# Last stage of a diffusion-step kernel: row moments on ScalarE, scale and finish on VectorE, inverse root on GpSimd

## The chip, the cores and the metric

The kernel runs on one core of one Trainium2 chip. A time is the device time of one execution in microseconds (us); the number to be forecast is the median over several executions. The core has TensorE (PE, matrix products, results in PSUM), VectorE (DVE), ScalarE (ACT), GpSimd (POOL), SyncE (SP, whose queue issues most of the DMAs) and 16 DMA engines. The engines run side by side, each works through its own instructions in order, and they wait for one another on semaphores.

## What is computed

One layer of a diffusion trunk on 1152 tokens (1024 latent, 128 context), width 1024, in float32. Cut to the parts that the change touches:

```python
def rms_norm(x, gain):
    y = xf * lax.rsqrt(jnp.mean(xf * xf, axis=-1, keepdims=True) + EPS)
    return (y * gain).astype(x.dtype)

def layer_norm(x, gain, bias):
    xc = xf - jnp.mean(xf, axis=-1, keepdims=True)
    var = jnp.mean(xc * xc, axis=-1, keepdims=True)
    return xc * lax.rsqrt(var + EPS) * gain + bias

hyo = rms_norm(hyo.reshape(B, L, HY_GROUPS, HY_GROUP_DIM), hy_out_gain)     # 8 groups of 64
x = layer_norm(DEEPNORM_ALPHA * x + g1 * mix, ln1_g, ln1_b)
moe = hier_moe(x * (1 + sc2) + sh2, ...)        # 2 of 32 experts for each token
x = layer_norm(DEEPNORM_ALPHA * x + g2 * moe, ln2_g, ln2_b)
```

## The kernel before

The tokens are nine tiles of 128 rows, eight latent (NLAT) and one context tile (NTILE = 9). The program runs through stages: modulation and projections, the Hyena convolution by Fourier matrices, the attention, the output projection with the first layer norm and the routing, a loop over blocks of 128 token rows through one expert each (33 blocks here), and the last stage, which adds each token's two expert rows to its residual and takes the second layer norm. Each engine's program is written out by hand in one function; nothing reorders it. `own` on VectorE, and `link` and `step` on GpSimd, issue one instruction and wait for its end before the next; `give` does the same on a named semaphore.

**Attention.** There are 72 rounds, eight heads for each of nine query tiles. In round i VectorE takes the maximum of the scores of round i + 1 (`maximum`, L1856), copies transposed probabilities out of PSUM (L1880) and, in round 8t + 7, takes the mean squares of the Hyena output of tile t: `mean_hyena`, one reduction of 512 columns to 8 sums (L1864) and one small operation (L1865). Its input, the squares, comes from ScalarE in round 8t + 4. In round 8t + 15 it also scales the attention output of tile t (`scale_attention`, L1527). GpSimd waits for the mean squares and for eight exponents (L636), then for ScalarE's copy of the attention's square sums (L639, round 8t + 11), takes the inverse roots in a chain of small steps (L642 to L648) and scales the Hyena rows (L651). TensorE turns the probabilities, multiplies with the values, and computes the scores of the next rounds, which wait until VectorE's maximum has freed their place in PSUM.

**Last stage.** SP waits until all expert rows are in HBM, then issues eight loads in four parts: tile 0, tiles 1 and 2, tiles 3 to 5, tiles 6 to 8. TensorE adds the two rows of a token by products with the identity, four for each tile of 128 x 1024, into one of four places `mixed(t)` in PSUM (AN = 4 places of two banks). VectorE adds ALPHA times x1 in place (`axpy`, L1540), takes the moments by two BatchNorm operations and an aggregation (L2081, L2082), and after every second tile takes the inverse roots of both in twelve small steps and one more for the bias (L2084, L1545, L1527, L1552, L1553, L2086). ScalarE then normalises from PSUM into one of three buffers `ynorm` (L1037) and thereby frees the place in PSUM. GpSimd multiplies with the gain and adds the bias (L751, L754) for the eight latent tiles; VectorE does so for the last. SP stores each tile to the output, and each buffer waits for its store before it is used again.

The last pair of expert products ends ahead of this stage, and between them and the first loaded tile TensorE has nothing to do.

## Time and profile before

| | us |
|---|---|
| median of 3 runs (1804.16 to 1805.94) | 1805.81 |
| the profiled execution | 1808.29 |
| its span on the page | 1806.1 |
| PE busy in the span | 1480.4 |
| DVE busy | 1015.0 |
| ACT busy | 358.9 |
| POOL busy | 365.7 |

The span runs from the first to the last instruction that the profile shows; the profiled execution took 2.2 us more than its span and 2.5 us more than the median. Changes are worked out as differences within the span and then taken off the median. A row of a timeline has its start, its duration, the engine and line, the operation with its output and input, how many instructions it merges, and in brackets the engine's idle time before it with what ended it. PSUM operands read PS, SBUF operands buffer.

### The profile page before, as it was taken

Reading aid. Unit: us, or ns where it says so; the run is one execution under the profiler, and the core shown is the slowest. Engines: PE = TensorE matmul, PEld = TensorE weight load, DVE = VectorE, ACT = ScalarE, POOL = GpSimd, SP = SyncE. Lnnn points to the kernel's source line nnn. Section 1 sums busy time; section 2 is a strip of 40 time slices with the busy share of each in tenths; the row PEclk is TensorE's granted clock in tenths of the full one; section 3 lists DMA queues with packets and bytes.
Section 4 is the critical chain, followed back from the end, with each engine's and each line's share of the span. In section 5 each row is a group of like instructions: output and inputs, shape, how many; then the busy total and the mean of one; then the engine's idle time right before and its main releaser. Section 6 shows DMA issues by size and latency. Waiting matters only on the chain.

```text
span 1806.1 us, 21613 instructions
## 1 busy us (share of the span) xinstructions
PE 1480.4 (82%) x8098; PEld 1008.3 (56%) x8098; DVE 1015.0 (56%) x1590; ACT 358.9 (20%) x665; POOL 365.7 (20%) x509
## 2 busy tenths in 40 slices
PE   7699998999974902924999997999469999999963
PEld 3466765444431401403888885455368888888821
DVE  3867882665538689587666662434533333333348
ACT  2544231111110100103565453000000000000001
POOL 0332030111100000000011114765212222222126
PEclk9799999999996955967999997999669999999986
DMA  9312203322311200202000003111248999998752
GB/s 302 135 58 80 85 30 134 117 94 94 117 64 37 83 13 19 75 12 103 1 2 2 1 2 140 58 59 47 93 167 318 325 334 329 333 339 315 248 232 88
DMA packets 96833, 229.50 MB, mean 127 GB/s; under 512 B 12439, under 2 KB 59095, under 8 KB 87992
## 3 DMA queue, kind: packets, MB, share of 16 engines
q1 hardware_dynamic: 72840, 195.14, 30.5%
q0 software_dynamic: 10960, 20.80, 3.3%
q10 hardware_dynamic: 12960, 12.59, 2.1%
q8 instruction: 46, 0.75, 0.2%
q14 instruction: 27, 0.22, 0.0%
HBM read 203.94 MB, written 40.01 MB: 135 GB/s over the span
## 4 chain that ended last, share of the span: by engine, by line
PE 68%; DVE 17%; DMA 4%; issue 4%; POOL 3%; ACT 3%; SPq 0%; ACTq 0%; DVEq 0%; POOLq 0%
PE PS L1047 57%; DVE buffer L1527 10%; PE PS L1050 6%; PE PS L1344 4%; DVE buffer L1540 2%; DMA buffer<-in_w_mod 2%; PE PS L1076 2%; POOL buffer L613 1%; POOL buffer L609 1%; DMA buffer<-expert_outputs 1%; DVE buffer L1856 1%; ACT buffer L977 1%; PE PS L1361 1%; ACT buffer L809 1%; DMA filter_spectra<-buffer 0%
## 5 line engine op out<-in xcount | busy, mean ns | idle before, releaser
L1047 PE MATMUL PS<-buffer 128*128 128x128 f32 (+5 forms) x5226 | 1235.4, 394 | 215.6 <-DVE buffer L1527 149.3
L1047 PEld LDWEIGHTS PS<-buffer 128*128 128x128 f32 (+1 forms) x5226 | 795.8, 197 | 627.4 <-issue 399.8
L1527 DVE TENSOR_TENSOR buffer<-buffer 128x512 f32<-128x512 f32 (+16 forms) x489 | 311.3, 637 | 28.2 <-ACT buffer L801 5.6
L1050 PE MATMUL PS<-buffer 128*128 128x128 f32 x1176 | 166.3, 284 | 63.7 <-DVE buffer L1527 53.5
L1527 DVE TENSOR_TENSOR buffer<-PS,buffer 128x1024 f32<-128x1024 f32 (+2 forms) x99 | 91.7, 927 | 188.8 <-PE PS L1047 168.2
L1050 PEld LDWEIGHTS PS<-buffer 128*128 128x128 f32 x1176 | 137.6, 155 | 93.8 <-issue 79.1
L1527 DVE TENSOR_TENSOR buffer<-buffer,PS 128x256 f32<-128x256 f32 (+3 forms) x53 | 27.4, 516 | 210.9 <-PE PS L1047 201.0
L1856 DVE TENSOR_SCALAR_CACHE_REDUCE buffer<-PS 128x1152 f32<-128x1152 f32 (+1 forms) x72 | 89.2, 1239 | 43.8 <-PE PS L1047 43.5
L944 ACT ACTIVATE buffer<-buffer 128x1152 f32<-128x1152 f32 (+1 forms) x72 | 83.7, 1163 | 109.8 <-DVE buffer L1856 109.8
L636 POOL TENSOR_TENSOR buffer<-buffer 128x8 f32<-128x8 f32 x9 | 1.8, 203 | 443.6 <-DVE buffer L1865 443.6
L1540 DVE SCALAR_TENSOR_TENSOR buffer<-buffer 128x512 f32<-128x512 f32 (+5 forms) x114 | 88.3, 774 | 3.9
L1025 ACT ACTIVATE buffer<-PS 128x256 f32<-128x256 f32 x33 | 12.7, 384 | 370.2 <-PE PS L1047 259.2
L1344 PE MATMUL PS<-buffer 128*64 128x128 f32 x1168 | 79.3, 279 | 6.4 <-ACT buffer L977 1.5
L1880 DVE COPY buffer<-PS 128x640 f32<-128x640 f32 x64 | 52.8, 825 | 55.0 <-issue 28.5
L1804 DVE TENSOR_SCALAR buffer<-PS,buffer 128x1024 f32<-128x1024 f32 (+1 forms) x24 | 21.0, 877 | 105.6 <-PE PS L1047 105.1
L1344 PEld LDWEIGHTS PS<-buffer 128*64 128x64 f32 x1168 | 62.6, 137 | 21.1 <-ACT buffer L977 15.2
L2061 DVE SCALAR_TENSOR_TENSOR buffer<-PS,buffer 128x1024 f32<-128x1024 f32 x33 | 42.4, 1284 | 40.5 <-PE PS L1047 40.5
L621 POOL TENSOR_TENSOR buffer<-buffer 2x256 f32<-2x256 f32 x16 | 12.0, 748 | 234.3 <-ACT buffer L779 234.3
L720 POOL COPY buffer<-buffer 128x1 int32 x32 | 5.9, 186 | 232.0 <-DVE buffer L2061 232.0
L2045 DVE COPY buffer<-PS 128x1024 f32<-128x1024 f32 x33 | 40.4, 1225 | 16.1 <-PE PS L1050 16.1
L711 POOL DMA_INDIRECT expert_outputs<-buffer x36 | 36.5, 1013 | 47.7 <-POOL buffer L720 25.5
L607 POOL TENSOR_TENSOR buffer<-buffer 128x256 f32<-128x256 f32 x8 | 8.7, 1088 | 174.3 <-ACT buffer L801 174.3
(150 smaller groups left out, 916.4 us busy)
## 6 DMA issues: line engine op xcount, KB each, us to landing
buffer<-in_exp_w_gate SPq DMA_DIRECT2D x33, 1024.0 KB
buffer<-in_exp_w_up SPq DMA_DIRECT2D x33, 1024.0 KB
buffer<-in_exp_w_down SPq DMA_DIRECT2D x33, 1024.0 KB
buffer<-in_w_mod SPq DMA_DIRECT2D x24, 1024.0 KB, 6.3
filter_spectra<-buffer ACTq DMA_DIRECT2D x88, 128.0 KB, 1.7
buffer<-filter_spectra SPq DMA_DIRECT2D x22, 512.0 KB, 3.6
buffer<-in_w_in SPq DMA_DIRECT2D x9, 1024.0 KB, 5.3
buffer<-expert_outputs SPq DMA_DIRECT2D x4, 1536.0 KB, 18.2
```

Source lines behind the costliest of these rows:

```text
L711: pool.indirect_dma_start(out=y_d[:, :], out_offset=bass.IndirectOffsetOnAxis(ap=rows, axis=0), in_=ybuf[:, s, :], in_offset=None, bounds_ ...
L944: act.activation(probs[:, i % 2, 0:n], probs[:, i % 2, 0:n], ACT.Exp, bias=nmax[:, i:i + 1], scale=-1.0, accum_out=psums[:, i:i + 1]).then ...
L1047: return nc.tensor.matmul(out, lhsT, rhs, start=start, stop=stop)
L1050: return nc.tensor.transpose(out, in_, ident)
L1076: last = nc.tensor.matmul(PS[32 * j:32 * j + 32, at:at + CHUNK], cond_wide[:, k, :], mod_weights(c)[:, k, :], start=half == 0, stop=half = ...
L1344: last = nc.tensor.matmul(PS[HD * u:HD * (u + 1), at:at + P], vals, probsT[:, (first + u) % 4, a, :], start=a == 0, stop=a == len(tiles) - ...
L1527: return dve.tensor_tensor(out, a, b, op)
L1540: own(dve.scalar_tensor_tensor(out, a, s, b, ALU.mult, op))
L1856: give(dve.tensor_scalar(probs[:, i % 2, 0:n], PS[:, 0:n], -1.0, None, ALU.mult, ALU.min, accum_out=nmax[:, i:i + 1]), "max_ready")
L1880: give(dve.tensor_copy(probsT[:, i % 4, 4:9, :], PS[:, 2048:2688].rearrange("p (t n) -> p t n", t=5)), "probsT_d")
L2045: dve.tensor_copy(xgT[:, s, :, :], PS[:, 0:1024].rearrange("p (k n) -> p k n", k=KT)).then_inc(sem("xT_ready"), 1)
L2061: dve.scalar_tensor_tensor(ybuf[:, s, :], PS[:, 2048:3072], row_scale[:, s, 0:1], row_gain, ALU.mult, ALU.mult).then_inc(sem("y_ready_to_s ...
```

## The change

In the attention, `mean_hyena` leaves VectorE. GpSimd waits for the squares and adds them up by halves, in six additions of 8 x 32, 8 x 16, 8 x 8, 8 x 4, 8 x 2 and 8 x 1 elements, followed by the small operation with 1/64 and EPS, all ahead of its wait for the exponents.

In the last stage:

- TensorE adds the residual of tiles 0 to 3, by two products each of a matrix ALPHA x identity with x1. These stand ahead of the waits for the loads. VectorE makes that matrix in the routing, in `upper`, by one operation on 128 x 128.
- VectorE adds the residual of tiles 4 to 8 as before (`add_residual`).
- ScalarE takes the moments: for each tile one Copy and one Square of 128 x 1024 from PSUM with an accumulated sum (`take_moments`). What they write is not read.
- VectorE computes (x - mean) x gain out of PSUM into the place of the loaded rows (`gain_rows`), which frees the place in PSUM for TensorE, and later multiplies with the inverse root and adds the bias, in SBUF (`finish_rows`).
- GpSimd takes the inverse roots in 17 small steps for each of the groups of tiles (0), (1, 2), (3, 4), (5, 6); VectorE those of tiles 7 and 8.
- The outputs are stored from the place of the loaded rows, so no buffer waits for a store.

```diff
             for t in range(NTILE):
                 v, r, tmp = (stat[:, i, 0:16] for i in range(3))
+                pool.wait_ge(sem("mix_squared"), t + 1)
+                y = mix_sq[:, 1, :].rearrange("p (g d) -> p g d", g=8)
+                n = HD // 2
+                while n > 1:
+                    link(pool.tensor_tensor(y[:, :, 0:n], y[:, :, 0:n], y[:, :, n:2 * n], ALU.add))
+                    n //= 2
+                link(pool.tensor_tensor(v[:, 8:16], y[:, :, 0], y[:, :, 1], ALU.add))
+                pool.sem_inc(sem("mix_meant"), 1)
+                link(pool.tensor_scalar(v[:, 8:16], v[:, 8:16], 1.0 / HD, EPS, ALU.mult, ALU.add))
                 pool.wait_ge(sem("exp_ready"), 8 * t + 8)
-                pool.wait_ge(sem("mix_meant"), t + 1)
...
+            for t0, t1 in GROUPS:
+                mean, square, v, r, tmp = (x[:, t0:t1] for x in (row_mean, row_square, row_var, row_scaling, row_tmp))
+                pool.wait_ge(sem("moments_taken"), 2 * t1)
+                step(pool.tensor_tensor(tmp, mean, mean, ALU.mult))
+                step(pool.tensor_tensor(v, square, tmp, ALU.subtract))
...
+                for scale in (1.0, 2.0, 16.0):
+                    step(pool.tensor_tensor(tmp, r, r, ALU.mult))
...
+            def take_moments(t):
+                if t < AN:
+                    act.wait_ge(sem("outputs_mixed"), t + 1)
+                else:
+                    act.wait_ge(sem("residual_added"), t - AN + 1)
+                if t:
+                    act.wait_ge(sem("moments_taken"), 2 * t)
+                act.activation(unread[:, 0, :], mixed(t), ACT.Copy, scale=1.0 / D, accum_out=row_mean[:, t:t + 1]).then_inc(
+                    sem("moments_taken"), 1)
+                act.activation(unread[:, 1, :], mixed(t), ACT.Square, scale=D ** -0.5, accum_out=row_square[:, t:t + 1]).then_inc(
+                    sem("moments_taken"), 1)
...
+            for t in (0, 1, 3, 2):
+                if t == 2:
+                    pe.wait_ge(sem("y_ready_to_send"), 2 * pairs + 2)
+                for h in range(2):
+                    mm(mixed(t)[:, 512 * h:512 * (h + 1)], upper, x1[:, t, 512 * h:512 * (h + 1)], True, False)
...
-                    pe.wait_ge(sem("ynorm_ready"), t - AN + 1)
+                    pe.wait_ge(sem("y_gained"), t - AN + 1)
...
+            def add_residual(t):
+                dve.wait_ge(sem("outputs_mixed"), t + 1)
+                dve.scalar_tensor_tensor(mixed(t), x1[:, t, :], ALPHA, mixed(t), ALU.mult, ALU.add).then_inc(sem("residual_added"), 1)
+
+            def gain_rows(t):
+                dve.wait_ge(sem("moments_taken"), 2 * t + 2)
+                dve.scalar_tensor_tensor(y_of(t), mixed(t), row_mean[:, t:t + 1], ln2_g, ALU.subtract, ALU.mult).then_inc(
+                    sem("y_gained"), 1)
+
+            def finish_rows(t):
+                dve.wait_ge(sem("y_gained"), t + 1)
+                dve.scalar_tensor_tensor(y_of(t), y_of(t), row_scaling[:, t:t + 1], ln2_b, ALU.mult, ALU.add).then_inc(
+                    sem("y_ready"), 1)
+
             dve.wait_ge(sem("ln2_loaded"), 32)
-            dve.wait_ge(sem("ynorm_ready"), NTILE)
-            own(tt(y, y, ln2_g, ALU.mult))
-            give(tt(y, y, ln2_b, ALU.add), "last_y_ready")
+            for t in range(NTILE):
+                if AN <= t:
+                    add_residual(t)
+                if t:
+                    gain_rows(t - 1)
+                if t in (3, 5, 7, 8):
+                    g = (3, 5, 7, 8).index(t)
+                    dve.wait_ge(sem("rows_scaling_ready"), g + 1)
+                    for done in range(*GROUPS[g]):
+                        finish_rows(done)
+            gain_rows(NLAT)
...
+            rsqrt(r, v, tmp)
+            for t in (NLAT - 1, NLAT):
+                finish_rows(t)
```

The order of VectorE's instructions in round 15 of the attention (tile 1) before the change. Rows give line, operation, output and input, and the semaphores waited for.

```order
L1880 COPY buffer<-PS 128x640 [waits attn_product,probs_transposed,max_ready]
L1864 TENSOR_REDUCE buffer<-buffer 128x8 [waits scales_ready,mix_squared,probsT_d]
L1865 TENSOR_SCALAR buffer<-buffer 128x8 [waits dve_step]
L1527 TENSOR_TENSOR buffer<-buffer,PS 128x512 [waits scales_spread,mix_meant]
L1856 TENSOR_SCALAR buffer<-PS 128x1152 [waits probs_transposed,scores_ready,attn_scaled]
```

And the same place after it (the helper line L1527 is now L1550, L1880 is L1894, L1856 is L1879):

```order
L1894 COPY buffer<-PS 128x640 [waits attn_product,probs_transposed,max_ready]
L1879 TENSOR_SCALAR buffer<-PS 128x1152 [waits probs_transposed,scores_ready,probsT_d]
L1894 COPY buffer<-PS 128x640 [waits attn_product,probs_transposed,max_ready]
L1550 TENSOR_TENSOR buffer<-buffer,PS 128x512 [waits scales_spread,probsT_d]
L1879 TENSOR_SCALAR buffer<-PS 128x1152 [waits probs_transposed,scores_ready,attn_scaled]
```

The reduction and the small operation are gone from between the copy and the next maximum.

VectorE in the last stage before the change, one tile and the inverse roots of a pair:

```order
L1540 SCALAR_TENSOR_TENSOR PS<-buffer,PS 128x1024 [waits outputs_mixed,dve_step]
L2081 BN_STATS buffer<-PS 128x6 [waits dve_step] x2
L2082 BN_AGGR buffer<-buffer 128x2 [waits dve_step]
L2084 TENSOR_SCALAR buffer<-buffer 128x2 [waits dve_step]
L1545 TENSOR_SCALAR buffer<-buffer 128x2 [waits dve_step]
L1527 TENSOR_TENSOR buffer<-buffer 128x2 [waits dve_step] x2
L1552 SCALAR_TENSOR_TENSOR buffer<-buffer 128x2 [waits dve_step]
```

And after it, from the residual of tile 5 to the residual of tile 7 (L2088 is `add_residual`, L2092 `gain_rows`, L2097 `finish_rows`):

```order
L2088 SCALAR_TENSOR_TENSOR PS<-buffer,PS 128x1024 [waits outputs_mixed]
L2092 SCALAR_TENSOR_TENSOR buffer<-PS,buffer 128x1024 [waits moments_taken]
L2097 SCALAR_TENSOR_TENSOR buffer<-buffer 128x1024 [waits y_gained,rows_scaling_ready]
L2097 SCALAR_TENSOR_TENSOR buffer<-buffer 128x1024 [waits y_gained]
L2088 SCALAR_TENSOR_TENSOR PS<-buffer,PS 128x1024 [waits outputs_mixed]
L2092 SCALAR_TENSOR_TENSOR buffer<-PS,buffer 128x1024 [waits moments_taken]
L2088 SCALAR_TENSOR_TENSOR PS<-buffer,PS 128x1024 [waits outputs_mixed]
```

The chain of small steps is gone from VectorE, and wide operations with waits for three other engines stand in its place.

TensorE at the end of the expert products, after the change; the wait for `yg_loaded0` is that for the first loaded tile:

```order
L1065 MATMUL PS<-buffer 128x512 [waits hidden_ready,y_ready_to_send]
L1065 MATMUL PS<-buffer 128x512 x9
L1516 REGISTER_ALU
L1065 MATMUL PS<-buffer 128x512 [waits y_ready_to_send]
L1065 MATMUL PS<-buffer 128x512
L1065 MATMUL PS<-buffer 128x512 [waits yg_loaded0]
L1065 MATMUL PS<-buffer 128x512 x3
```

Before the change the first row and three more products were followed at once by the wait for `yg_loaded0`; eight products now stand between.

## Rows read from the trace of the kernel before

**Rows 1.** The page: shares of the span in the chain that ended last.
```profile
PE 68%; DVE 17%; DMA 4%; issue 4%; POOL 3%; ACT 3%; SPq 0%; ACTq 0%; DVEq 0%; POOLq 0%
```

**Rows 2.** Timeline of DVE in the last stage, one pair of tiles.
```profile
1761.57 1.23 DVE L1540 SCALAR_TENSOR_TENSOR PS<-buffer,PS 128x1024 f32<-128x1024 f32 x1
...
1767.71 2.23 DVE L1545 TENSOR_SCALAR buffer<-buffer 128x2 int32<-128x2 int32 x1
1769.98 2.39 DVE L1527 TENSOR_TENSOR buffer<-buffer 128x2 f32<-128x2 f32 x2
...
1774.17 1.23 DVE L1540 SCALAR_TENSOR_TENSOR PS<-buffer,PS 128x1024 f32<-128x1024 f32 x1
```

**Rows 3.** Timeline of all engines in the last stage, POOL's row at that pair.
```profile
1767.57 2.35 POOL L751 TENSOR_TENSOR buffer<-buffer 128x1024 f32<-128x1024 f32 x1
```

**Rows 4.** The same timeline, the end of the program.
```profile
1798.15 1.20 ACT L1037 ACTIVATE buffer<-PS,buffer 128x1024 f32<-128x1024 f32 x1 [9.08 <-DVE buffer L2086]
1799.48 2.48 DVE L1527 TENSOR_TENSOR buffer<-buffer 128x1024 f32<-128x1024 f32 x2 [1.37 <-ACT buffer L1037]
1801.99 0.33 SPq L441 DMA_DIRECT2D out_ctx<-buffer  x1
```

**Rows 5.** The same timeline, PE: tiles 0 to 2, 3 to 4, one weight load.
```profile
1733.97 12.49 PE L1047 MATMUL PS<-buffer 128*128 128x512 f32 x24 [11.38 <-DMA buffer<-expert_outputs]
...
1748.19 7.13 PE L1047 MATMUL PS<-buffer 128*128 128x512 f32 x16 [1.73 <-DMA buffer<-expert_outputs]
...
1763.90 0.34 PEld L1047 LDWEIGHTS PS<-buffer 128*128 128x128 f32 x1 [0.52 <-issue]
```

**Rows 6.** Stretches of PE's work: busy us (count) by engine, granted clock, DMA share, GB/s.
```profile
1748.20:1758.80 10.60, 10.56 (x24) 4.47 (x24) 9.80 (x14) 2.30 (x2) 8.61 (x4) 1.00 0.64 258
1762.90:1768.80 5.90, 5.88 (x7) 2.51 (x8) 5.62 (x9) 0.97 (x1) 5.82 (x3) 0.52 0.06 24
```

**Rows 7.** Groups by line, shapes apart: busy us, mean ns | idle before.
```profile
L2061 DVE SCALAR_TENSOR_TENSOR buffer<-PS,buffer 128x1024 f32<-128x1024 f32 x33 | 42.4, 1284 | 40.5 <-PE PS L1047 40.5
L2057 DVE SCALAR_TENSOR_TENSOR buffer<-buffer 128x1024 f32<-128x1024 f32 x33 | 42.1, 1276 | 0.0
L1540 DVE SCALAR_TENSOR_TENSOR PS<-buffer,PS 128x1024 f32<-128x1024 f32 x9 | 11.1, 1229 | 16.8 <-PE PS L1047 16.6
L944 ACT ACTIVATE buffer<-buffer 128x1152 f32<-128x1152 f32 x64 | 80.5, 1258 | 104.2 <-DVE buffer L1856 104.1
L944 ACT ACTIVATION_READ_ACCUMULATOR buffer<-buffer 128x1 f32 x72 | 13.4, 186 | 0.0
```

**Rows 8.** Timeline of POOL in the attention: first and last of fourteen small steps.
```profile
898.79 0.20 POOL L642 TENSOR_SCALAR buffer<-buffer 128x16 int32<-128x16 int32 x1
...
902.83 0.26 POOL L648 TENSOR_SCALAR buffer<-buffer 128x16 f32<-128x16 f32 x1
```

**Rows 9.** Timeline of all engines early in the program: DVE beside POOL.
```profile
53.72 0.73 POOL L609 TENSOR_TENSOR buffer<-buffer 128x256 f32<-128x256 f32 x1
53.73 0.69 DVE L1527 TENSOR_TENSOR buffer<-PS,buffer 128x512 f32<-128x512 f32 x1 [0.81 <-ACT buffer L794]
...
54.83 2.02 DVE L1527 TENSOR_TENSOR buffer<-buffer 128x1536 f32<-128x1536 f32 x1
55.20 2.24 POOL L609 TENSOR_TENSOR buffer<-buffer 128x256 f32<-128x256 f32 x1
```

**Rows 10.** Chain of waits in the attention, a round without mean_hyena: start, us, what.
```profile
886.02 1.10 PE PS L1047 x6
```

**Rows 11.** Timeline of all engines in round 15.
```profile
913.14 0.69 DVE L1864 TENSOR_REDUCE buffer<-buffer 128x8 f32<-128x512 f32 x1
...
913.86 0.17 DVE L1865 TENSOR_SCALAR buffer<-buffer 128x8 f32<-128x8 f32 x1
...
916.21 1.37 PE L1047 MATMUL PS<-buffer 128*128 128x512 f32 x6 [0.35 <-DVE buffer L1856]
```

**Rows 12.** Waits in the attention: who waited for whom, us in total, times, longest.
```profile
POOL buffer L639 <- ACT buffer L963: 107.7, 9, 14.2
```

71 lines of the change are left out of this document (22 added, 49 removed).

## The prediction

> **What bounds the kernel now.** I read the chain that ended last first. Most of it is TensorE, whose work outside the places below the change leaves alone; the parts to watch are the 17% on VectorE [rows 1]. Then the timeline of the last stage. From tile 4 on, the last stage is VectorE's: a pair of tiles goes from 1761.57 to 1774.17, 12.6 us [rows 2]. The arithmetic is about 3 us for each tile, yet two small operations of 128 x 2 elements took 2.23 us and 2.39 us (for two) where such an operation takes 0.17 us [rows 2, 11]. The reader should see beside them that GpSimd's product with the gain started 0.14 us ahead of the first and lasted 2.35 us [rows 3]: VectorE's operation ended 0.02 us after it. TensorE has finished tile 5 by 1758.8 [rows 6], and the program still runs for 47 us, because a place in PSUM comes free only by way of VectorE's roots and ScalarE. The end is a chain without cover: ScalarE 1.20 us, VectorE two operations in 2.48 us, a store, 4.1 us from VectorE's end at 1801.96 to the end of the span [rows 4]. In the attention I looked at the round with `mean_hyena`: its reduction stands directly ahead of the maximum for which TensorE waits [rows 11].
>
> **The attention.** The edit takes 0.69 + 0.17 us and two gaps, 0.93 us, off VectorE between a copy and a maximum [rows 11]. TensorE stood idle there for 0.35 us before its next scores and took 1.37 us for them, where an undisturbed round has 1.10 us [rows 10, 11]; together 0.62 us. A maximum 0.93 us earlier ends ahead of TensorE's need, so both go. There are seven such rounds (15, 23, ... 63). In round 7 nothing is queued behind the reduction; in the last of the seven the products behind are short, so there only the 0.35. Sum: 6 x 0.62 + 0.35 = 4.1 us. The lower end is the visible idle time alone, 7 x 0.35 = 2.4 us; the upper end is all that leaves VectorE, 7 x 0.93 = 6.5 us. I take 4.1, since it is the difference of two measured rounds.
>
> GpSimd gets seven steps a tile. A 256-element addition took 0.73 us [rows 9], small steps come at (902.83 - 898.79) / 13 = 0.31 us [rows 8]; so about 0.8 + 0.5 + 5 x 0.33 = 3 us. The nearest cover is its wait for the copied sums, 107.7 us in nine waits, 12 us each [rows 12]. The scaling of tile t - 1 ends about a round after the squares are ready, and the sums come some six rounds later, so the 3 us cost nothing. For the context tile, whose rounds are short, the cover is smaller; by the order, the sums still come last, and I put the excess at 0 to 1 us once and take 0.
>
> **The routing.** ALPHA x identity is one more VectorE operation of 128 x 128, on the way to the first gather. Its nearest rows are 0.17 us for 8 columns and 1.28 us for 1024 [rows 7, 11]; I take 0.2 us, a loss.
>
> **The last stage, before tile 4.** Eight residual products follow the last expert product. A tile's four products are eight records, and 24 records took 10.6 us at full clock [rows 6], so 3.5 us a tile and 0.88 us a product: 7.1 us for eight. TensorE was idle for 11.38 us before the first tile [rows 5]; they fit into it. The first loaded tile starts at 1733.97 as before. Tiles 0 to 2 took 12.49 us, tile 3 waited for its load until 1748.19, and tile 4 was ready at 1748.19 + 7.13 = 1755.3 [rows 5]. None of that moves, since loads set it. Four residuals leave VectorE, but there it was not late.
>
> ScalarE needs two passes for each tile. The nearest rows: 1.20 us for 1024 columns from PSUM without a sum [rows 4], 1.26 us for 1152 columns and 0.19 us for reading the sum, mostly beside the pass [rows 7]. I take 1.3 us a pass, 2.6 us a tile, 23.4 us for nine. From tile 0 at 1739.5 it keeps ahead of VectorE. A new stage of waits arises: `gain_rows` waits for ScalarE, and behind it in VectorE's order stand finishes and residuals, and behind these the next moments. TensorE waits for `gain_rows(t - 4)`, which is long done.
>
> **The last stage, from tile 4.** VectorE is the bound. From 1755.4 it has 5 residuals (tiles 4 to 8), 6 gains (3 to 8) and 8 finishes (1 to 8), nineteen wide operations. Their kinds took 1.23, 1.28 and 1.28 us [rows 7]: 19 x 1.28 = 24.3 us with gaps. It waits 0.9 us for tile 5, mixed at 1758.8 [rows 6]. The roots of tiles 7 and 8 are 14 small steps at 0.2 us [rows 11], 2.8 us, without cover. GpSimd's root chains take 17 x 0.31 = 5.3 us each. The first three have 6 us or more until VectorE wants them. The fourth starts with tile 6's moments at 1767.5 and is wanted at 1773.9, and in between stand two finishes. Those read two SBUF operands. The trace has such a case: beside a VectorE operation with two SBUF inputs a GpSimd addition took 2.24 us, beside one with a PSUM input 0.73 us [rows 9]. So the two finishes hold GpSimd up for about 2.2 us: 1767.5 + 5.3 + 2.2 = 1775.0, a wait of 1.1 us. Add 0.3 us for finishes that a small step holds up. VectorE's end: 1755.4 + 24.3 + 0.9 + 2.8 + 1.1 + 0.3 = 1784.8. The tail was 4.15 us; now two stores follow at 1.3 us, for which I add 0.4 (0 to 1.3): 1789.3. That is 16.8 us less than 1806.1.
>
> The Trainium skill ("SBUF — State Buffer", section "Who interferes with whom") says that a VectorE instruction with two SBUF inputs contends with a GpSimd instruction that reads SBUF, and one with at most one SBUF input, outside the two-port modes, does not. Rows 9 agree: 2.24 us against 0.73 us. By that rule only the finishes hold GpSimd; without it the fourth chain would be in time and the end 1.4 us earlier.
>
> **Sum.** 4.1 - 0.2 + 16.8 = 20.7 us. The span would be 1785.4 us, the median 1805.81 - 20.7 = 1785.1; I say 1785.
>
> **Rivals.**
>
> (a) The attention gives nothing: TensorE's next wait, for ScalarE's exponents, takes the place of the one removed, or GpSimd's reduction comes late. For: every round has such a wait. Against: rounds without the reduction are shorter by just the difference. 1805.81 - 16.6 = 1789.
>
> (b) GpSimd's chains become the bound. If every wide VectorE operation holds GpSimd, those with PSUM too, each small step waits for the end of one while VectorE is busy. In the fourth group five operations pass, so five steps; the other twelve take 12 x 0.31 = 3.7 us of stall instead of 1.1. In the third group eight operations pass and nine steps remain, 2.8 us. The steps in turn hold VectorE for some 0.2 us each, about 13 steps, 2.6 us. Together 8 us: 1793. Against it: 0.73 us beside a PSUM operand [rows 9].
>
> The Trainium skill ("Perfetto Trace Analysis", section "Optimizing Scalar/DVE Operations") warns that moving work between GpSimd and VectorE might not help, because they share a port. By rows 9 the price is a wait for two operations, which (b) sets at its worst.
>
> (c) ScalarE is the bound: a pass with a sum out of PSUM costs about twice its price, 2.5 us. Then 18 x 2.5 + 1 = 46 us from 1739.5, tile 8's moments at 1785.5, and 1.3 + 2.8 + 2.6 + 4.55 behind them: 1796.8, less 3.9: span 1792.9, median 1792.6. Against: 1.26 us for more columns [rows 7]. No row has the sum out of PSUM. Below 2 us a pass it is hidden for the most part.
>
> (d) Slower: TensorE's clock. Between 1762.9 and 1768.8, after a pause, the granted clock was 0.52, that is the lower level of 1.2 GHz, and a weight load came every 0.86 us [rows 5, 6], so 6.9 us a tile. If it stayed at that level from the last expert product to the end, the residual products end at 1722.6 + 13.8 = 1736.4, nine tiles at 1798.5, and behind them 16.2 us (a residual, two gains, two finishes, 2.8 of roots, two finishes, the tail): 1814.7, less 3.9 of the attention is 1810.8, the median 1810. It turns at 6.4 us a tile: above that the kernel is slower than before. For: pauses bring the low level. Against: with places freed early TensorE works without a pause from 1748.2, and it kept 1.00 there [rows 6].
>
> **How the numbers follow.** The forecast has 0.64, (a) 0.13, (b) 0.10, (c) 0.07, (d) 0.06. Ends of the forecast: 2.4 us more in the attention, 1.1 without the stall, 0.4 in the tail and 0.8 in nineteen operations make 1780.4; 1.7 us less in the attention and 1.9 in tail and context tile make 1788.7. The range reaches down to 1779 for small gaps that I can't see, and up to 1794 for (b) and (c); (d) lies outside. A difference of about 0.2%, 3.6 us, is what a measurement of this kernel can tell from none. Faster by more: all but (d), 0.94; of (d), 0.04 slower and 0.02 within.
>
> **What would show it.** In the attention the nine reductions and small operations are gone from VectorE, and TensorE's idle time before the scores of rounds 15 to 63 is gone; a span of eight rounds shrinks by 0.6 us. GpSimd's wait for the copied sums falls from 12 to 9 us a tile. In the last stage VectorE shows nineteen wide operations nearly back to back, TensorE ends near 1769 less the 4 us gained earlier, and the last store is issued about 17 us sooner after tile 3's arrival. In (b) VectorE waits for GpSimd's last step three times for over 2 us; in (c) ScalarE's passes exceed 2 us; in (d) the granted clock is near 0.5 beyond tile 3. I am wrong at the root if VectorE has long idle time between tile 4 and the end.

## The result and the profile after

The changed kernel takes 1782.22 us in the median of four runs (1779.21 to 1783.8), the kernel before, run beside it, 1804.99 us (1804.04 to 1805.94). The ratio is 0.9872 [0.9855, 0.9889], 22.8 us less. The forecast was 1785 us, 20.7 us less. The profiled execution took 1783.76 us, with a span of 1781.9 us where it was 1806.1 us: 24.2 us less in the two traces, which this section divides up.

The page of the changed kernel: span, busy time by engine, and the shares in the chain that ended last, which answers to [rows 1].

```profile
span 1781.9 us, 21717 instructions
...
PE 1480.1 (83%) x8114; PEld 1009.4 (57%) x8114; DVE 980.7 (55%) x1510; ACT 367.3 (21%) x692; POOL 367.4 (21%) x624
...
PE 70%; DVE 14%; DMA 4%; issue 4%; POOL 4%; ACT 3%; SPq 0%; ACTq 0%; DVEq 0%; POOLq 0%
```

TensorE's busy time is what it was, 1480.1 us against 1480.4. VectorE's fell by 34 us and its share of the chain from 17% to 14%.

**Three stretches.** The last scaling of an expert's output on VectorE started at 1722.73 before and starts at 1719.11 now. First the row of before, then that of after, each from the timeline:

```profile
1722.73 1.28 DVE L2061 SCALAR_TENSOR_TENSOR buffer<-PS,buffer 128x1024 f32<-128x1024 f32 x1 [2.75 <-PE PS L1047]
```

```profile
1719.11 1.28 DVE L2074 SCALAR_TENSOR_TENSOR buffer<-PS,buffer 128x1024 f32<-128x1024 f32 x1 [2.75 <-PE PS L1065]
```

From there to the end of the span are 83.4 us before and 62.8 us after: the last stage gives **20.6 us**. Ahead of it lie 3.6 us: the attention gives **4.0 us**, 0.1 us is there before it, and the part between the attention and the last stage takes 0.6 us back.

**The attention.** The chain of waits from round 15 on, after the change (start, us, what), answers to [rows 10, 11]:

```profile
913.27 1.31 PE PS L1362 x20
914.59 1.13 PE PS L1068 x9
915.72 1.11 PE PS L1065 x6
...
920.22 1.31 PE PS L1362 x20
```

The scores take 1.11 us where they took 1.37 us behind 0.35 us of idle time, and the two rounds from one L1362 row to the next take 6.95 us where they took 7.56 us. The products themselves were no slower before: the timeline gives these six 1.37 us before and 1.35 us after. After a stop, though, their start does not lie beside the end of the products ahead, while now they start at 915.48 and the products ahead end at 915.72; that is where the other quarter of a microsecond comes from. VectorE's timeline in that round no longer has the reduction:

```profile
912.14 0.82 DVE L1894 COPY buffer<-PS 128x640 f32<-128x640 f32 x1 [0.77 <-DVE buffer L1879]
912.99 0.69 DVE L1550 TENSOR_TENSOR buffer<-buffer,PS 128x512 f32<-128x512 f32 x1
913.72 1.36 DVE L1879 TENSOR_SCALAR_CACHE_REDUCE buffer<-PS 128x1152 f32<-128x1152 f32 x1
```

**The last stage, up to tile 4.** Timeline of the changed kernel: TensorE's loaded tiles (they answer to [rows 5]) and ScalarE's two passes for tile 0.

```profile
1730.27 5.40 PE L1065 MATMUL PS<-buffer 128*128 128x512 f32 x8 [4.43 <-DMA buffer<-expert_outputs]
1735.71 1.02 ACT L1054 ACTIVATE buffer<-PS 128x1024 f32<-128x1024 f32 x1 [24.23 <-PE PS L1065]
1736.63 0.19 ACT L1054 ACTIVATION_READ_ACCUMULATOR buffer<-PS 128x1 f32 x1
1736.72 1.01 ACT L1056 ACTIVATE buffer<-PS 128x1024 f32<-128x1024 f32 x1
1736.82 7.13 PE L1065 MATMUL PS<-buffer 128*128 128x512 f32 x16 [1.15 <-DMA buffer<-expert_outputs]
1744.52 20.87 PE L1065 MATMUL PS<-buffer 128*128 128x512 f32 x48 [0.57 <-DMA buffer<-expert_outputs]
```

TensorE still waits for the loads ahead of tiles 0, 1 and 3. The residual products shorten its idle time before tile 0 from 11.38 us to 4.43 us and move nothing: tile 3 starts 25.4 us after the last scaling, as before (1748.19 - 1722.73 = 25.5). From tile 3 on TensorE works in one piece and has mixed all nine tiles at 1765.4.

**From tile 4.** Timeline of VectorE in the changed kernel; the third and the fifth row answer to [rows 2], the last to [rows 4]:

```profile
1751.69 1.23 DVE L2088 SCALAR_TENSOR_TENSOR PS<-buffer,PS 128x1024 f32<-128x1024 f32 x1 [3.07 <-PE PS L1065]
1752.83 1.28 DVE L2092 SCALAR_TENSOR_TENSOR buffer<-PS,buffer 128x1024 f32<-128x1024 f32 x1
1755.12 1.23 DVE L2088 SCALAR_TENSOR_TENSOR PS<-buffer,PS 128x1024 f32<-128x1024 f32 x1 [1.02 <-PE PS L1065]
...
1757.46 2.47 DVE L2097 SCALAR_TENSOR_TENSOR buffer<-buffer 128x1024 f32<-128x1024 f32 x2
...
1762.17 1.22 DVE L2088 SCALAR_TENSOR_TENSOR PS<-buffer,PS 128x1024 f32<-128x1024 f32 x1
...
1769.96 2.48 DVE L2097 SCALAR_TENSOR_TENSOR buffer<-buffer 128x1024 f32<-128x1024 f32 x2 [0.67 <-POOLq L768]
1772.36 1.28 DVE L2092 SCALAR_TENSOR_TENSOR buffer<-PS,buffer 128x1024 f32<-128x1024 f32 x1
1773.55 0.35 DVE L1550 TENSOR_TENSOR buffer<-buffer 128x2 f32<-128x2 f32 x2
...
1776.32 2.48 DVE L2097 SCALAR_TENSOR_TENSOR buffer<-buffer 128x1024 f32<-128x1024 f32 x2
```

From the residual of tile 5 to that of tile 7, a pair, 7.05 us pass (1755.12 to 1762.17) where a pair took 12.6 us [rows 2]. In the 27.1 us from 1751.69 to 1778.80 VectorE waits twice, 1.02 us for tile 5 and 0.67 us for GpSimd's fourth chain; the roots of the last two tiles take 2.77 us; the other 22.65 us are nineteen wide operations. GpSimd beside the first of the double finishes (timeline of GpSimd, same kernel):

```profile
1757.42 0.20 POOL L763 TENSOR_TENSOR buffer<-buffer 128x2 f32<-128x2 f32 x1
1757.69 1.09 POOL L764 TENSOR_TENSOR buffer<-buffer 128x2 f32<-128x2 f32 x1
1758.87 1.13 POOL L765 TENSOR_SCALAR buffer<-buffer 128x2 f32<-128x2 f32 x1
1760.09 0.20 POOL L766 TENSOR_TENSOR buffer<-buffer 128x2 f32<-128x2 f32 x1
```

Two steps last 1.09 and 1.13 us while VectorE finishes rows (1757.46 to 1759.93). Beside the residual at 1759.85, which reads one operand from PSUM, a step takes 0.20 us.

### The profile page after: what moved, and what is told of

It is laid out like the page before. It is cut to its first block, busy times and chain, and to the rows that moved or that the text cites. A ratio compares the mean times of both kernels' runs of the same rounds, so it can differ in the third digit from the quotient of the medians.

```text
span 1781.9 us, 21717 instructions
## 1 busy us (share of the span) xinstructions
PE 1480.1 (83%) x8114; PEld 1009.4 (57%) x8114; DVE 980.7 (55%) x1510; ACT 367.3 (21%) x692; POOL 367.4 (21%) x624
## 4 chain that ended last, share of the span: by engine, by line
PE 70%; DVE 14%; DMA 4%; issue 4%; POOL 4%; ACT 3%; SPq 0%; ACTq 0%; DVEq 0%; POOLq 0%
PE PS L1065 58%; DVE buffer L1550 9%; PE PS L1068 6%; PE PS L1362 4%; DVE buffer L1563 2%; DMA buffer<-in_w_mod 2%; PE PS L1094 2%; POOL buffer L613 1%; POOL buffer L609 1%; DMA buffer<-expert_outputs 1%; ACT buffer L991 1%; PE PS L1379 1%; DMA filter_spectra<-buffer 1%; ACT buffer L823 1%; ACT buffer L958 1%
## 5 line engine op out<-in xcount | busy, mean ns | idle before, releaser
L1550 DVE TENSOR_TENSOR buffer<-buffer 128x512 f32<-128x512 f32 (+15 forms) x471 | 300.2, 637 | 26.1 <-ACT buffer L815 5.6
L1550 DVE TENSOR_TENSOR buffer<-PS,buffer 128x1024 f32<-128x1024 f32 (+2 forms) x99 | 91.8, 927 | 189.3 <-PE PS L1065 168.7
L1550 DVE TENSOR_TENSOR buffer<-buffer,PS 128x256 f32<-128x256 f32 (+3 forms) x53 | 27.3, 515 | 211.8 <-PE PS L1065 201.0
L1879 DVE TENSOR_SCALAR_CACHE_REDUCE buffer<-PS 128x1152 f32<-128x1152 f32 (+1 forms) x72 | 89.2, 1239 | 41.1 <-PE PS L1065 40.7
L637 POOL TENSOR_TENSOR buffer<-buffer 128x256 f32<-128x256 f32 (+4 forms) x45 | 17.8, 396 | 365.2 <-ACT buffer L964 361.7
L1039 ACT ACTIVATE buffer<-PS 128x256 f32<-128x256 f32 x33 | 12.6, 383 | 370.3 <-PE PS L1065 370.3
L1894 DVE COPY buffer<-PS 128x640 f32<-128x640 f32 x64 | 52.8, 825 | 60.3 <-issue 30.1
L1362 PE MATMUL PS<-buffer 128*64 128x128 f32 x1168 | 79.3, 279 | 6.7 <-ACT buffer L991 1.8
L1362 PEld LDWEIGHTS PS<-buffer 128*64 128x64 f32 x1168 | 62.6, 137 | 21.4 <-ACT buffer L991 15.6
L2074 DVE SCALAR_TENSOR_TENSOR buffer<-PS,buffer 128x1024 f32<-128x1024 f32 x33 | 42.4, 1284 | 40.5 <-PE PS L1065 40.5
L719 POOL DMA_INDIRECT expert_outputs<-buffer x36 | 36.3, 1007 | 47.7 <-POOL buffer L728 25.5
```

Source lines behind the costliest of these rows:

```text
L719: pool.indirect_dma_start(out=y_d[:, :], out_offset=bass.IndirectOffsetOnAxis(ap=rows, axis=0), in_=ybuf[:, s, :], in_offset=None, bounds_ ...
L1362: last = nc.tensor.matmul(PS[HD * u:HD * (u + 1), at:at + P], vals, probsT[:, (first + u) % 4, a, :], start=a == 0, stop=a == len(tiles) - ...
L1550: return dve.tensor_tensor(out, a, b, op)
L1879: give(dve.tensor_scalar(probs[:, i % 2, 0:n], PS[:, 0:n], -1.0, None, ALU.mult, ALU.min, accum_out=nmax[:, i:i + 1]), "max_ready")
L1894: give(dve.tensor_copy(probsT[:, i % 4, 4:9, :], PS[:, 2048:2688].rearrange("p (t n) -> p t n", t=5)), "probsT_d")
L2074: dve.scalar_tensor_tensor(ybuf[:, s, :], PS[:, 2048:3072], row_scale[:, s, 0:1], row_gain, ALU.mult, ALU.mult).then_inc(sem("y_ready_to_s ...
```

## The experiments

"Last stage" is here always the time from the start of the last scaling on VectorE to the end of the span, in the profiled execution of each kernel. The ratio is that to the kernel before.

| run | ratio [95%] | last stage, us |
|---|---|---|
| kernel before | 1 | 83.4 |
| the change | 0.9872 [0.9855, 0.9889] | 62.8 |
| attention part alone | 0.9986 [0.9975, 0.9996] | 83.5 |
| last-stage part alone | 0.9884 [0.9865, 0.9903] | 63.0 |
| change, residuals on VectorE | 0.9874 [0.9855, 0.9894] | 62.8 |
| before, without GpSimd's wide work | 0.9896 [0.9879, 0.9912] | 63.7 |
| change, roots on VectorE | 0.9912 [0.9891, 0.9932] | 70.3 |
| change, TensorE kept busy | 0.9875 [0.9849, 0.9901] | 61.6 |
| change, six load parts | 0.9856 [0.9829, 0.9882] | 61.2 |
| both of these | 0.9847 [0.982, 0.9875] | 58.9 |
| before, gain and bias on VectorE | 0.9986 [0.9971, 1.0] | 82.6 |
| both, residuals of 7 and 8 on TensorE | 0.9823 [0.98, 0.9845] | 59.0 |
| the change again | 0.9859 [0.9837, 0.9881] | 62.7 |
| both, residuals of 7 and 8 on TensorE, other root groups | 0.9829 [0.9804, 0.9854] | 58.9 |

Single executions of one kernel lie up to 7 us to either side of its median (1800.01 against 1807.15 us for the kernel before), which is more than several of the differences asked about. The last stage repeats within some 0.3 us, unless a load lands at another time; so the small questions are answered by stretches of the traces.

The attention does not repeat as well. From its first maximum to the last spreading of the scales it took 267.4 to 267.7 us in the four kernels with VectorE's reduction, but 262.6 to 264.8 us in the ten without. Nearly all of that spread lies in its first eight rounds. They took 26.6, 27.6 or 28.6 us, and in their first 8 us the granted clock was 1.00, 0.79 or 0.57. From the ninth maximum on, the attention took 240.1 to 240.3 us with the reduction and 236.1 to 236.4 us without, in all fourteen traces. The whole times of two kernels can therefore differ by 2 us through TensorE's clock there, and the ratios carry that.

### Which part gives what: each alone

The attention part in the kernel before (the six additions on GpSimd, the call removed on VectorE; the last stage as in the kernel before):

```diff
+                pool.wait_ge(sem("mix_squared"), t + 1)
+                y = mix_sq[:, 1, :].rearrange("p (g d) -> p g d", g=8)
...
-                pool.wait_ge(sem("mix_meant"), t + 1)
```

> The kernel before, with only the attention part of the change: GpSimd adds up the Hyena squares, VectorE's reduction is gone. My theory: TensorE's 0.35 us idle and the slower next scores in rounds 15 to 63 go, 6 x 0.62 + 0.35 = 4.1 us less than before, ratio 0.9977; the last stage keeps its length of 83.4 us from the last scaling of expert outputs to the end. Rival (a): the next wait takes its place, 0 to 1 us less, ratio 1.000.

Measured: 0.9986 [0.9975, 0.9996], 2.5 us less (0.7 to 4.5). The stretch from the first maximum to the last spreading of the scales took 263.7 us, where it took 267.7 us before: 4.0 us. The whole program's interval agrees with that, but is wide. What makes the 4.0 us firm is that the first eight rounds took the same in both traces (27.64 and 27.66 us), so all of it lies in the rounds behind them, where each of the fourteen traces shows it. The last stage is untouched, 83.5 us. Rival (a), that the attention gives nothing, is out.

The last-stage part in the kernel before:

```diff
-            for t0 in range(0, NTILE, 2):
-                tiles = range(t0, min(t0 + 2, NTILE))
...
+            for t in range(NTILE):
+                if AN <= t:
+                    add_residual(t)
+                if t:
+                    gain_rows(t - 1)
```

> The changed kernel with VectorE's reduction back in the attention, so only the last stage (and the product matrix in the routing) is changed. My theory: the last stage alone shortens the span by about 20.3 us (20.6 seen from the last scaling of expert outputs to the end, less 0.3 for the matrix), ratio about 0.9888; and this together with the attention-only kernel adds up to the whole change. Rival: part of the last stage's gain is a side effect of another start (phase of clock or of transfers), then it differs from 20 us by more than 3.

Measured: 0.9884 [0.9865, 0.9903], 20.9 us less; last stage 63.0 us, attention stretch 267.6 us. The two parts are independent, and their times add up: 4.0 + 20.4 us in the stretches, against 4.0 + 20.6 us for both at once.

### The residuals of tiles 0 to 3 on VectorE

```diff
-            for t in (0, 1, 3, 2):
-                if t == 2:
-                    pe.wait_ge(sem("y_ready_to_send"), 2 * pairs + 2)
-                for h in range(2):
-                    mm(mixed(t)[:, 512 * h:512 * (h + 1)], upper, x1[:, t, 512 * h:512 * (h + 1)], True, False)
...
             for t in range(NTILE):
-                if AN <= t:
-                    add_residual(t)
+                add_residual(t)
```

> The changed kernel with the residual of tiles 0 to 3 on VectorE as well, and no residual products on TensorE. Theory 1: VectorE was idle before tile 4, so only tile 3 matters: its moments come 1.2 us later, and the end moves by 0 to 1.3 us; ratio to the changed kernel within 0.001. Theory 2: the products keep TensorE's clock up before the first tile, so that without them the first tiles come later and the end moves by more than 2 us. It shows as the granted clock in the first tile.

Measured: 0.9874 [0.9855, 0.9894] and 62.8 us. The eight residual products are worth nothing here; VectorE has time for these four residuals while the loads arrive. They do not warm TensorE either: its first loaded tile took 5.4 us at a granted clock of 0.63 after 11.28 us of idle time, and 5.40 us at 0.68 with the residual products and 4.43 us of idle time.

### What the kernel before lost to GpSimd

GpSimd's two products of 1024 columns become products of 2 columns. The kernel leaves out the rest of the gain and bias of the eight latent tiles; everything else is the kernel before.

```diff
-                pool.tensor_tensor(y, y, ln2_g, ALU.mult).then_inc(sem("pool_step"), 1)
+                pool.tensor_tensor(y[:, 0:2], y[:, 0:2], ln2_g[:, 0:2], ALU.mult).then_inc(sem("pool_step"), 1)
...
-                pool.tensor_tensor(y, y, ln2_b, ALU.add).then_inc(sem("y_ready"), 1)
+                pool.tensor_tensor(y[:, 0:2], y[:, 0:2], ln2_b[:, 0:2], ALU.add).then_inc(sem("y_ready"), 1)
```

> The kernel before, in which GpSimd leaves out nearly all of the last gain and bias of the eight latent tiles (2 columns of 1024 instead of all), so those outputs are not the layer norm's. It asks what GpSimd's wide operations cost VectorE by blocking its small ones. Theory 1: the blocks (about 2.0 us twice in each pair from tile 3 on, three times in the last tile) are all that goes; VectorE's last stage shrinks by about 4 x 2.05 + 2.0 x 5 = 16 to 18 us, to a ratio of about 0.991. Theory 2: small operations are slow for another reason (waits for their own completion), then less than 3 us go.

Measured: 0.9896 [0.9879, 0.9912], last stage 63.7 us. With nothing else changed, 19.7 of the change's 20.6 us are there. The timeline of VectorE in this kernel has the operations of [rows 2]:

```profile
1756.67 1.23 DVE L1540 SCALAR_TENSOR_TENSOR PS<-buffer,PS 128x1024 f32<-128x1024 f32 x1
...
1762.82 0.17 DVE L1545 TENSOR_SCALAR buffer<-buffer 128x2 int32<-128x2 int32 x1
1763.02 0.35 DVE L1527 TENSOR_TENSOR buffer<-buffer 128x2 f32<-128x2 f32 x2
...
1765.18 1.23 DVE L1540 SCALAR_TENSOR_TENSOR PS<-buffer,PS 128x1024 f32<-128x1024 f32 x1
```

The operations that took 2.23 and 2.39 us take 0.17 and 0.35 us, and a pair takes 8.5 us instead of 12.6. The 4.1 us of difference are the two stalled operations (2.23 + 2.39 - 0.17 - 0.35 = 4.1): GpSimd's wide products cost VectorE that much in each pair. Over the whole stage, VectorE's last operation ends 60.6 us after the last scaling instead of 79.2 us, 18.6 us sooner. The other 1.0 us lies behind that operation: the end of the span follows after 3.1 us instead of 4.1. Its cause stands with the tail below.

### Is it then enough to take the work off GpSimd?

The kernel before, with gain and bias on VectorE for all tiles, one pair behind:

```diff
+            def finish(t):
+                y = ynorm[:, t % YN, :]
+                dve.wait_ge(sem("ynorm_ready"), t + 1)
+                own(tt(y, y, ln2_g, ALU.mult))
+                give(tt(y, y, ln2_b, ALU.add), "y_ready")
...
+                for t in range(max(t0 - 2, 0), t0):
+                    finish(t)
+            finish(NLAT)
```

> The kernel before with the last gain and bias of all tiles on VectorE instead of GpSimd, the pair before while the next pair's roots are done; everything is computed. Theory 1: the sixteen operations of 1.24 us (19.8 us) that come to VectorE take the place of the blocks of about 20 us that go, so the last stage is 83 us within 3, as before: freeing VectorE's small steps of GpSimd pays only because the change also takes the moments and four residuals off VectorE. Theory 2: the blocks cost more than they show and the last stage gets 5 us or more shorter.

Measured: 0.9986 [0.9971, 1.0], last stage 82.6 us. The timeline of VectorE in this kernel, the finishes of one pair:

```profile
1771.92 5.00 DVE L1518 TENSOR_TENSOR buffer<-buffer 128x1024 f32<-128x1024 f32 x4
1776.96 1.23 DVE L1531 SCALAR_TENSOR_TENSOR PS<-buffer,PS 128x1024 f32<-128x1024 f32 x1
```

The small steps are short again, but four wide operations in 5.0 us stand in the place of 4.1 us of stall. Moving the work to VectorE as it is gains next to nothing. The change gains because it also leaves VectorE less work in a pair: the moments go to ScalarE, the roots to GpSimd, and gain and bias ride in two operations a tile that subtract the mean and multiply with the root anyway.

### The roots on VectorE

```diff
-                    dve.wait_ge(sem("rows_scaling_ready"), g + 1)
+                    roots(*GROUPS[g])
```

> The changed kernel with all inverse roots on VectorE (14 small steps for each of the four groups) and none on GpSimd. Theory 1: VectorE is the bound from tile 5 on, so the chains of the groups (1, 2), (3, 4), (5, 6) add 2.8 us each to the last stage and the 0.7 us wait for GpSimd goes: 62.8 + 8.4 - 0.7 = 70.5 us, or 1 to 2 us less where a chain fills VectorE's idle time before tiles 4 and 5. Theory 2: freed of GpSimd's chains the finishes get shorter and make up for it; then less than 4 us are added.

Measured: 0.9912 [0.9891, 0.9932], last stage 70.3 us, 7.5 us more than with the change. In the timeline of this kernel a chain of roots goes from 1762.52 to 1765.29, 2.8 us, on VectorE:

```profile
1762.52 0.35 DVE L1536 TENSOR_TENSOR buffer<-buffer 128x2 f32<-128x2 f32 x2
...
1765.29 2.48 DVE L2083 SCALAR_TENSOR_TENSOR buffer<-buffer 128x1024 f32<-128x1024 f32 x2
```

Three such chains are 8.4 us, less the wait for GpSimd of 0.67 us: 7.7. GpSimd's chains are worth having. Rival (b), in which they cost 8 us, is out, since VectorE waits for them only once, for 0.67 us.

### TensorE's pause and the size of the load parts

Four extra products into the place of tile 2, which later products overwrite, fill part of the pause:

```diff
                 if t == 2:
                     pe.wait_ge(sem("y_ready_to_send"), 2 * pairs + 2)
+                    for _ in range(4):
+                        mm(mixed(t)[:, 0:512], upper, x1[:, t, 0:512])
```

> The changed kernel with four more products of 512 columns, whose result is overwritten, ahead of the residual of tile 2, so that TensorE works up to about the time at which tile 0 lands (its idle time there falls from 4.4 us to about 1). Theory 1: the granted clock of tile 0 rises from 0.68 to 1.00 and tile 0 takes 3.6 us instead of 5.4, but tile 1 waits for its load 1.8 us longer, so the last stage keeps its 62.8 us within 0.3. Theory 2: TensorE's clock in the first tile sets the end; then it is 1.5 to 1.9 us shorter.

Measured: 0.9875 [0.9849, 0.9901], last stage 61.6 us. TensorE's rows (timeline of this kernel):

```profile
1727.41 3.70 PE L1065 MATMUL PS<-buffer 128*128 128x512 f32 x8 [1.12 <-DMA buffer<-expert_outputs]
...
1732.60 1.98 PE L1065 MATMUL PS<-buffer 128*128 128x512 f32 x4 [1.48 <-DMA buffer<-expert_outputs]
```

Tile 0 took 3.70 us at a granted clock of 1.00 instead of 5.40 us at 0.68, and then TensorE waited 1.48 us for tile 1. From tile 3's start to the end 37.4 us pass, as with the change. The 1.2 us that the stage is shorter come from a load: tile 3, for which TensorE waited 0.53 us here too, started 24.1 us after the last scaling, where it took 25.3 to 25.6 us in the nine other traces with four load parts. Whether the extra products have to do with that is not tested; it is one trace.

The loads in six parts instead of four:

```diff
-        YG_PARTS = ((0, 1), (1, 3), (3, 6), (6, 9))
+        YG_PARTS = ((0, 1), (1, 2), (2, 3), (3, 4), (4, 6), (6, 9))
...
```

> The changed kernel with the loads of the expert rows in six parts instead of four: tiles 0, 1, 2, 3, 4 to 5, 6 to 8. In the changed kernel TensorE waits 1.15 us for tile 1 and 0.57 us for tile 3. Theory: VectorE starts its residual of tile 4 that much earlier and the last stage is 1.7 us shorter, 61.1 us. Rival: the earlier first store slows the loads of tiles 6 to 8, or more issues on the queue delay them by 4 x 0.45 us, and nothing is left.

Measured: 0.9856 [0.9829, 0.9882], last stage 61.2 us, 1.6 us less than with the change. From tile 0 on TensorE has no wait for a load.

Both edits together:

> Both: six parts and the four products that keep TensorE busy. Theory 1: tile 0 takes 3.6 us, tile 1 is there by then, TensorE runs through from tile 0, and the last stage is 1.7 + 1.8 = 3.5 us shorter than the changed kernel's, 59.3 us. Theory 2: VectorE's work from tile 0 on, or the loads of tiles 6 to 8, bound it sooner; then it is no shorter than with six parts alone.

Measured: 0.9847 [0.982, 0.9875], last stage 58.9 us, 3.9 us less than with the change. Timeline of TensorE in this kernel, all nine tiles in one piece:

```profile
1726.82 31.17 PE L1066 MATMUL PS<-buffer 128*128 128x512 f32 x72 [1.06 <-DMA buffer<-expert_outputs]
```

The products that fill the pause gain nothing while a load is waited for anyway; once the loads come in time, they gain 2.3 us more (61.2 to 58.9), and that is TensorE: its nine tiles take 31.17 us in one piece, where six load parts alone took 33.40 us from the same start, 11.2 us after the last scaling. The whole times tell less, since the attention's first eight rounds took 28.6 us in the one trace and 26.6 us in the other.

### Less for VectorE, twice

On top of both edits, TensorE adds the residual of tiles 7 and 8 too:

```diff
+                if t >= 7:
+                    for h in range(2):
+                        mm(mixed(t)[:, 512 * h:512 * (h + 1)], upper, x1[:, t, 512 * h:512 * (h + 1)], True, False)
...
-                if AN <= t:
+                if AN <= t < 7:
                     add_residual(t)
```

> The kernel with six parts of loads and a busy TensorE, in which the residuals of tiles 7 and 8 too are added by TensorE. Theory 1: VectorE is the bound and loses two operations, TensorE ends 3.5 us later but still in time: the last stage is 1.5 to 2.4 us shorter than the 58.9 us of six parts with a busy TensorE, about 57 us, ratio to the kernel before about 0.983. Theory 2: tile 8, now later by 3.5 us, sets the end; then 0 to 1 us longer.

Measured: 0.9823 [0.98, 0.9845] with a last stage of 59.0 us. The ratio is the lowest, but its interval overlaps that of the kernel without this edit, and the stage shows no gain: the 2 us were missed. VectorE does leave out two operations, and then waits (timeline of VectorE in this kernel):

```profile
1753.76 1.28 DVE L2098 SCALAR_TENSOR_TENSOR buffer<-PS,buffer 128x1024 f32<-128x1024 f32 x1 [1.00 <-ACT buffer L1057]
...
1760.43 2.48 DVE L2103 SCALAR_TENSOR_TENSOR buffer<-buffer 128x1024 f32<-128x1024 f32 x2 [1.80 <-POOLq L769]
```

It waits 1.00 us for ScalarE's moments of tile 6. ScalarE starts on them at once when VectorE's residual of tile 6 is there, but the residual of tile 7, which covered them before, is no longer in between. And it waits 1.80 us for GpSimd's fourth chain, which was 0.67 us late already. A further kernel, otherwise the same, makes that chain one tile smaller and gives tile 6 to VectorE's own:

```diff
-        GROUPS = ((0, 1), (1, 3), (3, 5), (5, 7))
+        GROUPS = ((0, 1), (1, 3), (3, 5), (5, 6))
```

> The kernel with six parts, a busy TensorE and the residuals of tiles 7 and 8 on TensorE, in which GpSimd's fourth chain has tile 5 alone and VectorE's last chain has tiles 6, 7 and 8. In the kernel with the pair (5, 6) VectorE waited 1.8 us for GpSimd's fourth chain. Theory 1: that chain now starts one tile earlier and is in time, VectorE's own chain costs as much for three columns as for two, and the last stage is 59.0 - 1.8 = 57.2 us. Theory 2: three finishes behind VectorE's chain let the last stores queue, or VectorE waits for ScalarE's moments of tile 8 instead; then less than 1 us goes.

Measured: 0.9829 [0.9804, 0.9854], last stage 58.9 us, again no gain. In the timeline of VectorE the wait of 1.00 us for tile 6 is still there, the wait for GpSimd is down to 0.36 us, and a wait of 1.34 us for the moments of tile 8 has come:

```profile
1765.37 1.29 DVE L2103 SCALAR_TENSOR_TENSOR buffer<-buffer 128x1024 f32<-128x1024 f32 x1 [0.36 <-POOLq L769]
...
1768.00 1.28 DVE L2098 SCALAR_TENSOR_TENSOR buffer<-PS,buffer 128x1024 f32<-128x1024 f32 x1 [1.34 <-ACT buffer L1057]
```

ScalarE's pass for tile 8 in the same kernel (timeline of all engines):

```profile
1765.84 1.02 ACT L1055 ACTIVATE buffer<-PS 128x1024 f32<-128x1024 f32 x1 [3.03 <-PE PS L1066]
```

So ScalarE is not the slow one there. It had been idle for 3.03 us and started when TensorE had mixed tile 8, which was 45.8 us after the last scaling instead of 42.4 us with both edits alone, because TensorE now adds two residuals. The expectation had priced only VectorE's side of the move.

In the first of these kernels two operations, 2.3 us, were taken off VectorE and 2.1 us came back as waits (1.00 + 1.80 - 0.67). In the second the waits are 1.00 + 0.36 + 1.34 - 0.67 = 2.0 us, and the last of them is for TensorE.

### The change again

> The changed kernel again, for a comparison on the same chip with the version that has six parts, a busy TensorE and the last residuals on TensorE: ratio to the kernel before 0.987 within 0.002, last stage 62.8 us within 1.2 (the landing of the loads varied by that much between profiled runs).

Measured: 0.9859 [0.9837, 0.9881], last stage 62.7 us. The last stage repeats within 0.1 us, and the ratio of one and the same kernel came out as 0.9872 and as 0.9859: what lies between two of the ratios above by no more than that is not told apart by them.

## Why the prediction held, point by point

**The attention: right, 4.1 us against 4.0.** The removed wait was 0.35 us and the scores gave back the other 0.26. That the sum came out so close is in part luck: from the ninth maximum on, groups of eight rounds became shorter by 0, 0.60, 0.62, 0.36, 0.60, 0.63 and 0.60 us, and what follows them by 0.65 us. The prediction had 0.62 six times and 0.35 for the last; one of the six gave only 0.36 and the last 0.65. Why these two differ is not looked into. That GpSimd's seven steps are hidden was right as well: from 904.25 to 907.22 they take 3.0 us, as summed. But the sign that was named for it was wrong. Waits of GpSimd in the changed kernel (who for whom, us in total, times, longest):

```profile
POOL buffer L647 <- ACT buffer L977: 149.6, 9, 20.0
```

The wait for the copied sums rose from 12 to 16.6 us a tile [rows 12] instead of falling to 9. Before, GpSimd's wait for the mean ended at about 914, and only then could it handle the exponents, which were ready earlier; now it takes these at 908.00, some 6 us sooner (both in round 15), and waits all that longer for the sums. I had looked at the work added and not at the wait taken away on the same engine.

**The routing and what follows: about right.** ALPHA x identity takes 0.23 us on VectorE, the forecast was 0.2. The stretch between the attention and the last stage is 0.6 us longer than before; over all fourteen traces it varies from 600.6 to 603.1 us, so the rest of it has no cause in the change that I can name.

**The last stage: right in its mechanism, 3.8 us short in size**, 16.8 us against 20.6. Up to the residual of tile 4 the sum held: it starts 7.2 us after tile 3, as forecast, and the residual products lie in TensorE's pause. Behind it, the terms were:

| term of the sum | taken, us | measured, us |
|---|---|---|
| nineteen wide operations | 24.3 | 22.65 |
| wait for tile 5 | 0.9 | 1.02 |
| wait for GpSimd's fourth chain | 1.1 | 0.67 |
| roots of tiles 7 and 8 | 2.8 | 2.77 |
| finishes held by a small step | 0.3 | 0 |
| VectorE's end to the end of the span | 4.55 | 3.1 |

The last store was issued 34.3 us after tile 3's start instead of 53.8 us, 19.5 us sooner where about 17 had been named.

Two terms were mis-sized. The first, by 1.65 us, is "nineteen wide operations: 19 x 1.28 with gaps". Rows of 1.28 us start 1.20 us behind one another (1756.26 to 1757.46), rows of 1.23 us 1.14 us (1751.69 to 1752.83), where no instruction waits for the end of the one before: 22.65 / 19 = 1.19 us. The Trainium skill ("Perfetto Trace Analysis", section "Optimizing Scalar/DVE Operations") says that the latency which a profile shows for an instruction contains a write acknowledgement that overlaps with the next instruction. The trace agrees, with 0.08 and 0.09 us for these two. I had taken durations where starts were wanted, and added gaps that the kernel before had only because `own` waits after each operation: there a residual of 1.23 us (L1540) is followed by the next operation 1.26 us after its own start (1761.57 to 1762.83), where the change's residual of 1.23 us is followed after 1.14 us.

The other, by 1.45 us, is the tail. After VectorE's last operation it was 4.1 us before and is 3.1 us now, though 0.4 us had been added for a second store. The second store cost nothing that shows: from the issue of the last store to the end of SyncE's wait for it 2.6 us pass before and 2.7 us after. The 1.0 us is GpSimd's. Each engine's queue ends with a DRAIN; here are those of GpSimd and SyncE (L152, duration in ns and start), first before, then after the change:

```profile
L152 POOLq DRAIN  x1: 10725/10725/10725, 1795.1 to 1795.1; - x1
L152 SPq DRAIN  x1: 13/13/13, 1804.8 to 1804.8; - x1
```

```profile
L152 POOLq DRAIN  x1: 8325/8325/8325, 1770.0 to 1770.0; - x1
L152 SPq DRAIN  x1: 13/13/13, 1781.7 to 1781.7; - x1
```

GpSimd's ends 8.3 to 8.4 us after its last operation in both (1797.52 to 1805.8 and 1769.88 to 1778.3). Before, that was 1.0 us later than SyncE, which had waited for the last store, and the span ended behind it; after the change SyncE comes last. In the kernel with the attention part alone GpSimd's DRAIN ends last too, at 1803.0, and the tail is 4.1 us. In the twelve traces without GpSimd's wide products it is 3.1 to 3.3 us, among them the kernel in which those products have 2 columns and the stores and their semaphores are as before. The prediction took the 4.1 us for the store's; the trace of the kernel before already had GpSimd as the last one.

**The stall of GpSimd's chain** came as forecast: only the finishes hold it. The prediction had two finishes hold it up by about 2.2 us together, and two steps of 1.09 and 1.13 us, which otherwise take 0.2 us each, are what the trace shows. That is 1.8 us, and the other steps came every 0.27 to 0.32 us, so the fourth chain took 6.6 us instead of 7.5 us, and the wait for it was 0.67 us instead of 1.1 us.

**The rivals.** (a), the attention gives nothing: false by 4.0 us. (b), GpSimd's chains bound: VectorE waits for them once, 0.67 us, and steps beside operations with a PSUM operand take 0.20 us. (c), ScalarE: a pass with its sum takes 1.02 us and reading the sum 0.19, partly beside it, 2.1 us a tile; I had taken 2.6, and its price was in fact lower than that of its nearest row [rows 4]. Only when more is taken off VectorE does VectorE wait for its moments, 1.00 us for tile 6, and for tile 8 1.34 us, where ScalarE itself had waited for TensorE. (d), the half clock: stretches of the changed kernel (length, busy us and count by engine from PE to POOL, granted clock, DMA share, GB/s):

```profile
1730.30:1735.70 5.40, 5.37 (x8) 2.00 (x8) 0.00 (x0) 0.00 (x0) 0.00 (x0) 0.68 1.03 419
1744.50:1765.40 20.90, 20.87 (x48) 9.04 (x48) 15.17 (x13) 12.06 (x24) 11.24 (x40) 1.00 0.46 183
```

Tile 0 runs partly at the lower level of 1.2 GHz, 0.68 in the mean. From tile 3 to TensorE's end the clock is 1.00, 2.4 GHz. (d) is false, and the stretch of [rows 6] at 0.52 is gone together with the pauses that came before it.

**Why it was faster, shown and not shown.** Shown is that GpSimd's wide products cost the kernel before 19.7 us of its last stage, 18.6 us by holding VectorE's small steps and 1.0 us by GpSimd's late end, that their work on VectorE in the old form costs nearly as much again (63.7 to 82.6 us), that the roots on GpSimd are worth 7.5 us of the new form, and that the residual products are worth nothing. The moments on ScalarE were never run alone on either side; their part is argued from the two that were.

## What to carry to other kernels

When a small operation on VectorE lasts as long as a wide one on GpSimd beside it, price the block at the small operation's excess, here 4.1 us a pair, and compare that with the price of doing the work on VectorE: here that was 5.0 us a pair, so moving it alone was useless, and fusing it into operations that exist anyway was the gain. A sum over back-to-back operations goes by the distance of their starts, not by their durations. And where four engines share a stage, look at each one's slack before taking more off the bound: from 2.3 us taken off VectorE nothing was left, twice. ScalarE's moments and GpSimd's chain had lost the operations that covered them, and TensorE, which had taken the work over, came late with the last tile. At the end of the program, look at when each engine's queue ends, and not only at the last store.
